# Seven block products in place of eight in an attention projection, with the weight sums on GpSimd

## What is computed

```python
def attn_project(h, w_in):
    b, n, _ = h.shape
    q, k, v, g = jnp.split(h @ w_in, 4, axis=-1)
    ...
qs = apply_rope(qs, cos, sin)        # x * cos + rot(x) * sin
ks_ = apply_rope(ks_, cos, sin)
...
    return (o * jax.nn.silu(g)) @ w_out
```

## Time and profile before

| | |
|---|---|
| median of 3 executions | 2233.52 us (2232.45 to 2233.87) |
| the profiled execution's span | 2232.1 us |
| TensorE busy (matmuls) | 2169.6 us, 97% |
| VectorE / ScalarE / GpSimd busy | 1159.2 / 799.1 / 86.5 us |
| projection: q and k, gate units | about 675 to 1279 us |
| projection: value units | about 1279 to 1498 us |

### The profile page before, as it was taken

One profiled execution on the slowest core, in us unless ns is written; L12 is line 12 of the kernel. 1 busy time (PEld: TensorE's weight loads), 2 busy tenths in 40 slices (PEclk: granted clock), 3 DMA queues, 4 the chain that ended last, 5 costly groups with the idle time before them and its releaser, 6 DMA issues. The chain is left out here.

```text
span 2232.1 us, 33378 instructions
## 1 busy us (share of the span) xinstructions
PE 2169.6 (97%) x13623; PEld 2080.6 (93%) x13623; DVE 1159.2 (52%) x1776; ACT 799.1 (36%) x1454; POOL 86.5 (4%) x40
## 2 busy tenths in 40 slices
PE   8999999989999999999999999999999999999997
PEld 3999877989998999999999999999999999989997
DVE  4777464664245445544411132228888888875223
ACT  3511132233122112111321233336666666665110
POOL 0000000000000122112100000000000000000000
PEclk9999999989999999999999999999999999999999
DMA  8355343685234444765622544443444433308332
GB/s 332 137 175 174 124 146 104 250 306 161 75 130 135 141 122 131 204 155 130 167 90 80 216 162 165 157 164 134 161 161 161 159 141 114 121 1 264 114 128 85
DMA packets 124222, 339.22 MB, mean 152 GB/s; under 512 B 14272, under 2 KB 69696, under 8 KB 113856
## 3 DMA queue, kind: packets, MB, share of 16 engines
q1 hardware_dynamic: 124096, 337.46, 45.1%
HBM read 224.12 MB, written 113.25 MB: 151 GB/s over the span
## 5 line engine op out<-in xcount | busy, mean ns | idle before, releaser
L1776 PE MATMUL o_ps<-o_y_hi,o_w 128*128 128x384 f32 x1536 | 395.7, 337 | 14.8 <-DVE o_y_lo L1884 13.3
L1776 PEld LDWEIGHTS o_ps<-o_y_hi,o_w 128*128 128x128 f32 x1536 | 280.9, 190 | 16.3 <-DVE o_y_lo L1884 13.7
L866 PE MATMUL p_ps<-p_h_hi,p_w_hi 128*128 128x384 f32 x1152 | 267.5, 335 | 2.3 <-DVE p_xs L1091 2.3
L866 PE MATMUL p_ps<-p_h_hi,p_w_lo 128*128 128x384 f32 x1152 | 267.3, 335 | 0.0
L866 PE MATMUL p_ps<-p_h_lo,p_w_hi 128*128 128x384 f32 x1152 | 267.1, 335 | 0.0
L1776 PE MATMUL o_ps<-o_y_lo,o_w 128*128 128x384 f32 x768 | 258.7, 337 | 0.0
L866 PEld LDWEIGHTS p_ps<-p_h_hi,p_w_hi 128*128 128x128 f32 x1152 | 206.1, 188 | 2.6 <-issue 2.6
L866 PEld LDWEIGHTS p_ps<-p_h_lo,p_w_hi 128*128 128x128 f32 x1152 | 206.2, 188 | 0.0
L866 PEld LDWEIGHTS p_ps<-p_h_hi,p_w_lo 128*128 128x128 f32 x1152 | 206.1, 188 | 0.0
L2175 ACT ACTIVATE a_e<-a_ps,a_nmax 128x1152 f32<-128x1152 f32 x127 | 155.4, 1224 | 62.6 <-DVE a_nmax L2236 62.6
L2132 PE MATMUL a_ps<-a_v_hi,a_at_hi 128*128 128x256 f32 x576 | 173.0, 300 | 0.0
(11 more groups left out here) (263 smaller groups left out, 4055.4 us busy)
## 6 DMA issues: line engine op xcount, KB each, us to landing
p_w_raw<-w_in_dram SPq DMA_DIRECT2D x32, 1024.0 KB, 7.0
o_y_raw<-y_dram SPq DMA_DIRECT2D x96, 192.0 KB, 3.6
g_wada<-w_ada_dram SPq DMA_DIRECT2D x16, 1024.0 KB, 6.8
f_w_raw<-w_u_dram SPq DMA_DIRECT2D x32, 512.0 KB, 4.2
o_w_raw<-w_out_dram SPq DMA_DIRECT2D x32, 512.0 KB, 4.1
g_dram<-g_stage SPq DMA_DIRECT2D x16, 576.0 KB, 3.2
f_g<-g_dram SPq DMA_DIRECT2D x8, 1152.0 KB, 7.6
y_dram<-f_y SPq DMA_DIRECT2D x8, 1152.0 KB, 5.3
```

What stands on the lines that cost most here:

```text
L866: return pe.matmul(ps[:, 4 * b + c, 0:CH], a, x[:, c * CH:(c + 1) * CH], start=(d == 0 and j == 0), stop=(d == DT - 1 and j == 2))
L1776: mm = pe.matmul(ps[:, d, 0:CH], a, m, start=(e == 0 and j == 0), stop=(e == ET - 1 and j == 2))
```

## The change

For q, k and gate units from the second on, the first two token chunks are no longer multiplied as eight block products (2 blocks of columns x 2 halves of the input channels x 2 chunks, each 4 tiles x 3 passes = 12 matmuls) but as seven, by Winograd's form of Strassen's scheme: some products take sums of weight blocks against sums of token blocks, and the results are combined by adds. The third chunk stays as it was (`LATE`, 48 matmuls). Unit 0 and the value units multiply as before. In detail:

- The four sums of token blocks are made once, on GpSimd, at the start of the stage (128x1536 each), then cut by ScalarE and VectorE. GpSimd waits for the last stores of the stage before, since these tiles lie on its tiles.
- The four sums of weight blocks are made for each unit on GpSimd (`sums`, 128x512 each), then cut by ScalarE (two casts) and VectorE (`sums_lo`, two subtracts). `s_sum` and `s_lo` are the same SBUF, so each sum waits for the product that last read it.
- Weights have one buffer in place of two (`tiles.w[0]`), cut by halves: block 0 before the unit, block 1 after its start.
- The products of a unit are copied out of PSUM into `made_x` (ScalarE), and VectorE combines them there by five adds.
- Sine and cosine are now multiplied from SBUF, one instruction of 2304 elements each, one unit later; GpSimd's two rotations work on `made_x` and `turned`. `turned` and `cut_lo` are the same SBUF: sine waits for the low stores of the unit before (`lo_stored`).
- A gate unit's SiLU is applied in parts, after the combination for the first two chunks. Two token tiles are stored to DRAM and loaded back before the values, for room in SBUF. The q, k and gate loops are now written out, not loops of the program.

```diff
--- before.py
+++ after.py
...
+            def unit(n):
+                pe.wait_ge(w_lo_done, w_ready(n, 0))
+                pe.wait_ge(evicted, moved(n - 1, "near_near"))
+                product(Z1, weights(0, 0), quarter(0, 0), True, True).then_inc(proj_done, 1)
...
+                product(Z2, sums_of(1), mixed(1), True, True).then_inc(proj_done, 1)
+                pe.wait_ge(snapped, 2 * (n - 1) + 1)
+                product(Z1, weights(0, 1), quarter(1, 0), False, True).then_inc(proj_done, 1)
...
+                product(Z4, sums_of(2), mixed(2), True, True).then_inc(proj_done, 1)
...
+                product(Z3, sums_of(0), mixed(0), True, True).then_inc(proj_done, 1)
+                pe.wait_ge(w_lo_done, w_ready(n, 1))
...
+                pe.wait_ge(combined, summed(n, "third"))
+                product(Z4, weights(1, 1), mixed(3), False, True).then_inc(proj_done, 1)
+                pe.wait_ge(snapped, 2 * (n - 1) + 2)
+                product(Z3, sums_of(3), quarter(1, 1), False, True).then_inc(proj_done, 1)
+                for b in range(2):
+                    pe.wait_ge(evicted, moved(n - 1, f"late{b}"))
+                    product(LATE[b], weights(b, 0) + weights(b, 1), quarter(0, 2) + quarter(1, 2), True, True).then_inc(proj_done, 1)
...
+            def sine(n):
+                dve.wait_ge(evicted, moved(n, "late1"))
...
+                    dve.wait_ge(lo_stored, 64 * n)
+                dve.scalar_tensor_tensor(turned[:], made_x[n % 2][:], SCALE if n < H else 1.0,
+                                         cs[:, 1:2, :].to_broadcast([P, 2, T]), ALU.mult, ALU.mult).then_inc(sined, 1)
...
+            def turned_lo(n, b):
+                dve.wait_ge(rotated, 2 * n + 2)
+                dve.wait_ge(cut_hi_done, 2 * n + b + 1)
+                dve.tensor_tensor(cut_lo[:, b, :], made_x[n % 2][:, b, :], cut_hi[:, b, :].bitcast(F32),
+                                  ALU.subtract).then_inc(cut_lo_done, 1)
...
+            for n in range(1, UNITS):
+                tiles.split_lo(dve, n, 1, w_ready(n, 1))
+                if n <= ROPE:
+                    sine(n - 1)
+                dve.wait_ge(snapped, 2 * (n - 1) + 1)
+                add(n, "second", near(n)[:, chunk(1)], Z2, near(n)[:, chunk(0)], "sixth")
+                if n <= ROPE:
+                    cosine(n - 1)
+                else:
+                    scale(n - 1)
+                dve.wait_ge(combined, summed(n, "second"))
+                add(n, "third", far(n)[:, chunk(0)], Z4, near(n)[:, chunk(1)], "seventh")
...
+                if n <= ROPE:
+                    turned_lo(n - 1, 0)
+                if n + 1 < UNITS:
+                    sums_lo(n + 1, 0)
+                if n <= ROPE:
+                    turned_lo(n - 1, 1)
...
+                tiles.split_lo(dve, n + 1, 0, w_ready(n + 1, 0))
+                if n + 1 < UNITS:
+                    sums_lo(n + 1, 1)
...
+            def sums(n, which):
+
+                for m in which:
+                    if n > 1:
+                        pool.wait_ge(proj_done, made(n - 1, ("fifth", "sixth", "seventh", "near_far")[m]))
+                        pool.wait_ge(s_lo_done, 2 * (n - 2) + 2)
...
+            for n in range(1, UNITS):
+                more = n + 1 < UNITS
+                if more:
+                    sums(n + 1, (2, 0, 1))
+                if n <= ROPE:
+                    rotate(n - 1, 0)
+                if more:
+                    sums(n + 1, (3,))
+                if n <= ROPE:
+                    rotate(n - 1, 1)
```

More of the change, by code:

```diff
@@ L763, in _, with near, far, chunk @@
+        own_out = [nc.alloc_semaphore(f"p1_own_out{s}") for s in range(2)]
+        v_stored = [nc.alloc_semaphore(f"p1_v_stored{s}") for s in range(2)]
+        block = ctx.enter_context(nc.Block())
+        def near(n):
+            return made_x[n % 2][:, 0, :]
+        def far(n):
+            return made_x[n % 2][:, 1, :]
+        def chunk(c):
+            return slice(c * CH, (c + 1) * CH)
         @block.sync
@@ new lines, in quarter, with mixed, product @@
+            def quarter(k, c):
+                return [tuple(tiles.half(part, c, 4 * k + i) for part in range(2)) for i in range(4)]
+            def mixed(m):
+                return [(t_hi[m][:, i, :], t_lo[m][:, i, :]) for i in range(4)]
+            def product(bank, left, right, first, stop):
+                for i, ((w_hi, w_lo), (x_hi, x_lo)) in enumerate(zip(left, right)):
+                    for j, (a, x) in enumerate(passes(w_hi, w_lo, x_hi, x_lo)):
+                        mm = pe.matmul(ps[:, bank, 0:CH], a, x, start=(first and i == 0 and j == 0),
+                                       stop=(stop and i == len(left) - 1 and j == 2), skip_group_check=True)
+                return mm
@@ L936, in own_attention @@
                     mm.then_inc(own_back, 1)
-            loops(pe, body, first=by_chunk)
+            inverse_rms.sums(pe)
+            whole()
+            for n in range(1, UNITS):
+                unit(n)
+            for j in range(H):
+                values(j)
         @block.scalar
         def _(act):
-            for b in range(2):
-                act.sem_inc(drained[b], 1)
-                act.sem_inc(stored[b], 1)
-            act.sem_inc(proj_done, 1)
-            act.sem_inc(rotated, 1)
@@ new lines, in sums_lo, with add @@
+            def sums_lo(n, pair):
+                dve.wait_ge(s_summed, 4 * n)
+                dve.wait_ge(s_hi_done, s_ready(n, pair))
+                both = slice(2 * pair, 2 * pair + 2)
+                dve.tensor_tensor(s_lo[:, both], s_sum[:, both], s_hi[:, both].bitcast(F32), ALU.subtract).then_inc(s_lo_done, 1)
+            def add(n, event, into, bank, to, ready):
+                dve.wait_ge(proj_done, made(n, ready))
+                dve.tensor_tensor(into, ps[:, bank, 0:CH], to, ALU.add).then_inc(combined, 1)
@@ L1052, in past_split @@
-                dve.tensor_tensor(past_lo[:, :], past_raw[:, :], past_hi[:, :].bitcast(F32),
-                                  ALU.subtract).then_inc(past_lo_done, 1)
-            def after(kind):
-                if rope is not None and kind <= 1:
-                    past_split(kind)
-            inverse_rms.invert(dve)
-            for m in range(2 * DT, len(STEPS) + 1):
-                if m < len(STEPS):
-                    norm(m)
-                if m > 2 * DT:
-                    low_half(m - 1)
@@ L1100, in own_attention @@
+            for half in range(2):
+                tiles.split_lo(dve, UNITS, 1, v_ready(0) - 1 + half, rows=slice(4 * half, 4 * half + 4))
+            scale(UNITS - 1)
             def own_attention(n, at):
@@ L1130, in _ @@
         @block.gpsimd
         def _(pool):
-            def body(k, i, last):
-                for p in range(2):
-                    n = 2 * i + p
-                    for b in range(2):
-                        pool.wait_ge(drained[1], k["drain"][1] + n + 1)
-                        pool.wait_ge(stored[b], k["stored"][b] + 16 * k["stores"] * n)
-                        pool.tensor_tensor(stage[:, b, :], xs[:, 2 * b, :], xs[:, 3 - 2 * b, :],
-                                           ALU.add if b else ALU.subtract).then_inc(rotated, 1)
@@ new lines, in rotate @@
+            def rotate(n, b):
+                pool.wait_ge(cosined, n + 1)
+                x = made_x[n % 2][:, b, :]
+                pool.tensor_tensor(x, x, turned[:, 1 - b, :], ALU.add if b else ALU.subtract).then_inc(rotated, 1)
+            sums(1, (2, 0, 1, 3))
+            for n in range(1, UNITS):
+                more = n + 1 < UNITS
[5 more added lines that the diff above has]
+                    sums(n + 1, (3,))
+                if n <= ROPE:
+                    rotate(n - 1, 1)
```

816 lines of the change are left out of this document (484 added, 332 removed).

## The result

| | before | changed | ratio (95% interval) |
|---|---|---|---|
| median | 2233.47 us | 2277.84 us | 1.0201 (1.0187 to 1.0215) |
| the profiled execution's span | 2232.1 us | 2274.7 us | |

The account below looks back on a forecast made before the run. TensorE's count of matmuls was taken to bound the kernel before. Units +14.7, start +12 and values +4 gave +30.7 us on the 2232.1 span, the median 1.4 longer: 2264 us, range 2230 to 2296.

Parts of the forecast that it names:

- this case: Whole kernel, with VectorE and GpSimd taking turns by instruction: 2264 us, bounds about 2248 to 2286, chance 0.42.
- Matmuls and gate units: Projection stage: 276 fewer matmuls, 47.8 us if TensorE never stands; seven gate units at 22.97 us, together 160.8.
- A sum of GpSimd: GpSimd's weight sum of 512 elements in each unit: 1.25 us, bounds 1.19 and 2.68.
- The tail: Rope unit from product five through sums, rotations, cuts and weights: at least 25.1 us, so the matmul saving is lost there.
- R: End of a rope unit's second rotation: 19.8 us into the unit, 21.0 with turns at the port.
- The stores: Sine waits for the previous unit's low-cut store: landing at R + 9.6, sine 4.3 us into the next unit, 5.5 in k.
- The port: VectorE and GpSimd sharing one port in rope units: q unit 26.3 us, k unit 27.4, rope total 427.9.
- turns by instruction: Shared port of VectorE and GpSimd: the engines alternate instruction by instruction; chance 0.42.
- GpSimd always wins: Rival at the shared port: VectorE's cosine gives way to GpSimd's sums, q unit 27.7 us, total 2285; chance 0.28.
- The clock: TensorE's clock falling behind rope-unit waits: 1.7 us each, 27 us if all, 2291; chance 0.08 with other added waits.
- The start: Before unit 1: GpSimd's token sums hold VectorE's last chunk, unit 1 at 717 us, not 704.94: +12.
- The values: Start of the value units: bare weight pieces 1.5 us, ScalarE's stand for the last gate store 2.5 (0.5 to 6): +4.

Follow-up runs that it names:

- e6: Changed kernel with the low store that sine waits for made early, low part of block 1 left out, new_k stored last: 2280.70 us.
- e12: Changed kernel with the edits of e5 and e6 together, but new_k's stores back behind the high ones: 2241.88 us.
- e5: Changed kernel with VectorE's rest of the first pair of weight sums behind the next unit's weight half in rope units: 2277.07 us.
- e7: Changed kernel with GpSimd's two rotations ahead of all four weight sums in rope units, ScalarE and VectorE following: 2215.89 us.
- e4: Changed kernel with the four token sums on VectorE ahead of its late chunk instead of on GpSimd: 2269.23 us.
- e3: Changed kernel with the second value unit's weights cut behind the first value unit's fifth token tile: 2267.02 us.
- e8: Changed kernel with e7, e3 and e4, plus first weight half and PSUM copies earlier at the start, unit 1's third sum ahead of cosine: 2199.71 us.
- e13: Changed kernel with the edits of e7, e3 and e4 together: 2196.75 us.
- e9: Changed kernel with GpSimd's sum of two weight blocks made a copy of the second block, one SBUF input: 2242.09 us.

## Why the prediction was right, point by point

The forecast was 2264 with 2230 to 2296, slower at 0.78; measured 2277.84. The direction and the range held, the forecast was 14 us low. (The upper bound of this case, 2286, lies 2 us above what its own terms give, 2264 and 20.)

- **Matmuls and gate units: right.** 276 fewer; the gate units took 160.98 us, forecast 160.8.
- **A sum of GpSimd: right.** 1.25 taken, 1.30 measured alone (779.99). The line through the Trainium skill's figure (GPSIMD Engine Reference, Elementwise — side-by-side cycle accounting), an estimate of 1.38, was 0.08 too long, mine 0.05 too short.
- **The tail: right, and shown.** 25.1 was worked out, 25.13 measured in e6 where no store held sine. With turns, R was put at 21.0 and measured at 21.03 (764.82 less 743.79), the tail 5.2 against 4.95, the q unit 26.3 against 25.98. That the tail binds was shown by e12 with e5 and e6, and by e7.
- **The stores: right for k, 1 us short for q.** From R to sine 9.6 and 10.7 us were forecast; the means are 10.6 and 10.7. Sine was forecast 4.3 and 5.5 into the next unit; it began 4.6 to 6.8 (mean 5.5) in q and 5.3 to 6.0 (mean 5.7) in k units. e5 and e12 show that this loop is a limit of its own.
- **The port: turns by instruction, as forecast; "GpSimd always wins" fell.** Sine kept 2.55 us in all 16 units, but nothing of GpSimd ran beside it. Cosine met a sum in 14: in the eleven where it began first it kept 2.55 and the sum took up to 3.67, in the three where the sum was already running cosine itself took 3.48 to 3.55. Whoever comes second waits; likewise the add with two SBUF operands (L1292) takes 0.56 alone and 1.17 as its median. The Trainium skill's rule (GPSIMD Engine Reference, Specifications) on VectorE instructions with two SBUF inputs agrees with the trace: the combining adds, with one operand in PSUM, kept their time in all 92, also inside rotations. These are the changed kernel's rows, first a timeline's (the sum had begun at 966.37), then ns min/median/max:

```profile
966.53 3.55 DVE L1250 SCALAR_TENSOR_TENSOR p_made<-p_made,p_cs 128x2304 f32<-128x2304 f32 x1
...
L1234 DVE TENSOR_TENSOR p_made<-p_ps,p_made x92: 544/558/558, 723.2 to 1299.5; 128x384 f32<-128x384 f32 x92
...
L1292 DVE TENSOR_TENSOR p_made<-p_made x23: 558/1172/1698, 730.0 to 1295.9; 128x384 f32<-128x384 f32 x23
```

- **The clock: mis-sized, in the rope term.** I wrote that most waits would be split or under 3.2 us and so a fall was "an addition, not the rule". Waits of 1.96 to 2.41 us were followed by half clock in ten of the rope units behind the first (in eight at the unit's start, in two in its middle). A fall costs 1.58 us (e6); in the changed kernel the two q units without one took 25.98 and 25.66, the six with one 26.7 to 27.9. The 16 units came to 430.85 against 427.9: the k units took 27.0 and not 27.4, the q units 26.7 and not 26.3, the first 27.9 and not 25.7, behind a 6.8 us wait. That this term missed by only 3.0 is partly luck, for two errors offset each other. Units without a fall were shorter than forecast (q 25.8 on average, not 26.3; k 26.6, not 27.4), some 9 us over the stage; the first unit and the ten falls, priced at nothing in the sum, put some 12 back.
- **The start: right.** Unit 1 at 715.9, forecast 717. Four short VectorE operations took 10.75 us beside GpSimd's token sums of 3.5 (forecast 3.5). e4 moved these sums and won 8.6.

```profile
678.64 3.49 POOL L1366 TENSOR_TENSOR p_t_sum<-p_x,p_t_sum 128x1536 f32<-128x1536 f32 x1
...
680.09 10.75 DVE L1195 SCALAR_TENSOR_TENSOR p_x_late<-p_x_late,mod,ss 128x256 f32<-128x256 f32 x4 [6.16 <-ACT ss L106]
```

- **The values: the step that failed in size.** I put 1.5 for the bare weight pieces and 2.5 (0.5 to 6) for ScalarE's stand at the last gate store; they were 1.44 and 11.1, beyond the 8 us that the prediction named as the sign of a wrong term. The step let three free banks, 8.6 us, cover ScalarE's stand but for 2.5. The two stores are issued from 1310.49 on, behind sixteen loads for both attentions and one of the values' weights (1 MB), and landed 9.6 and 10.8 us after their issue; ScalarE stood 12.80 us, to 1322.11. That the loads made them late is read from the order in the queue; no run moved the loads. Behind its wait came the cast of a whole unit (1.90) and VectorE's subtract (2.29) before the first bank was free: 4.6 us more, to 1326.72, which the step left out. To TensorE's 7.97 us come 3.1 for the half clock behind it. e3 removed just that, 10.8 us.

By this the miss adds up: values +8.5, rope +3.0, the attention's first products +1.5, gate +0.2, start -1.1: 12.1, the span's 2274.7 against the 2262.6 forecast for it. The rest of the 14 is that the median lies 3.1 us above the profiled span, not 1.4.

What stays open: which of two equal waits is followed by half clock (796.43 with 1.96 us was; 743.79, 932.02 and 1092.36 with 1.96 were not, nor 1012.55 with 2.34), and what sets the two courses of e8 and e13.

## What to carry to other kernels

When an engine is given new work, find the piece that several loops share and put the new work behind it, not in it. Here the same sums, moved behind two rotations, turned a kernel 2.0% slower into one 0.8% faster, and 1.6% with two more moves. When one limit is removed and nothing happens, remove the second one too before giving up the theory. Cost a new wait for a store by what stands in the queue ahead of it there, not by the median landing elsewhere, and count what stands behind a wait that is moved. And when a sum of terms comes out near, look whether each term did: here a clock that fell ten times was hidden by waits that were priced too long.

## What the runs showed of the hardware

GpSimd and VectorE (with two SBUF inputs) take turns by instruction, and whichever comes second waits (cosine 2.55 us when first, 3.55 when second, beside a weight sum); a GpSimd instruction with one SBUF input takes part (0.61 us alone, up to 2.96 in e9), a VectorE add with one operand in PSUM does not (558 ns at most in 92). TensorE's granted clock fell to half behind many waits of no more than 2 us (in e6 behind six of eight of 1.96), at 1.58 us each. With TensorE never standing it was 0.51 from 717.57 to 721.00, behind a wait of 6.46 us, and 1.00 for the 364 us from there to 1085.00 (e7).
